# Layer 0 of a hybrid diffusion backbone: modulation dots at other places, convolution tiles in another order, and one scan group in another bank

## The reference, cut to what matters

```
sh1, sc1, g1, sh2, sc2, g2 = split(silu(c) @ ada_w[i] + ada_b[i], 6)
x = layer_norm(ALPHA * x + g1 * mixer(x * (1 + sc1) + sh1))
x = layer_norm(ALPHA * x + g2 * peer_ffn(x * (1 + sc2) + sh2))
```

## Time and profile before

| | |
|---|---|
| Median of three runs | 2045.37 us (2044.3 to 2049.02) |
| Profiled execution | 2046.35 us |
| its span | 2044.5 us |
| mean granted TensorE clock | 0.959 |
| PE busy | 1725.1 us (84%) |
| DVE busy | 1505.0 us (74%) |
| ACT busy | 603.1 us (29%) |
| DMA | 326 GB/s over the span |

### The profile page before, as it was taken

How to read it: one execution, slowest core, us unless ns; L and a number is a source line. 1 busy time by engine, 2 the same in 40 slices (tenths; PEclk the granted TensorE clock), 3 DMA queues, 4 the chain that set the end, 5 groups by cost and what they waited for, 6 DMA issues and landing times.

```text
span 2044.5 us, 18024 instructions
## 1 busy us (share of the span) xinstructions
PE 1725.1 (84%) x5374; PEld 970.2 (47%) x5374; DVE 1505.0 (74%) x3522; ACT 603.1 (29%) x1424; POOL 486.7 (24%) x516
## 2 busy tenths in 40 slices
PE   5998988988789976898899899969788877777776
PEld 5777467765445432343343578645344433332232
DVE  7899995767577767898886576666677777877755
ACT  2654661422222222333232121012222222232221
POOL 0000000003233333343333000013233333333331
PEclk9999998989999999999999899989999999999999
DMA  8244216738999999999999674549999999999996
GB/s 328 85 152 157 83 46 227 270 138 351 420 420 420 418 410 419 363 395 411 408 420 418 264 297 167 201 181 379 419 419 420 414 418 405 395 420 420 419 415 262
DMA packets 94473, 668.13 MB, mean 327 GB/s; under 512 B 11271, under 2 KB 11560, under 8 KB 14504
## 3 DMA queue, kind: packets, MB, share of 16 engines
q0 software_dynamic: 73728, 536.90, 64.2%
q1 hardware_dynamic: 20648, 130.08, 16.8%
HBM read 665.82 MB, written 1.11 MB: 326 GB/s over the span
## 4 chain that ended last, share of the span: by engine, by line
PE 35%; DMA 31%; DVE 15%; issue 2%; ACT 2%; PEldq 0%; POOL 0%; PEld 0%; DVEq 0%; SPq 0%; POOLq 0%; ACTq 0%
DMA expert_rows<-in_p_uv,chosen_experts 30%; PE bank L924 18%; DVE dot_products L1927 5%; PE bank L998 4%; PE bank L892 4%; PE bank L835 2%; PE bank L814 2%; PE bank L1074 1%; ACT weight_diagonal L1325 1%; PE bank L1038 1%; PE bank L1027 1%; DVE modulation_products L1457 1%; DVE scores L1885 1%; PE bank L953 1%; DMA weight_block<-in_m_in_blocks 0%
## 5 line engine op out<-in xcount | busy, mean ns | idle before, releaser
L924 PE MATMUL bank<-expert_rows,weight_diagonal 128*128 128x512 f32 x2048 | 972.6, 619 | 206.7 <-ACT weight_diagonal L1325 205.8
L1927 DVE SCALAR_TENSOR_TENSOR dot_products<-expert_rows,bank 128x1024 f32<-128x1024 f32 x512 | 625.1, 1221 | 314.1 <-DMA expert_rows<-in_p_uv,chosen_experts 304.9
L1103 POOL DMA_INDIRECT expert_rows<-in_p_uv,chosen_experts x512 | 486.5, 950 | 1529.4 <-PE bank L924 819.9
L924 PEld LDWEIGHTS bank<-expert_rows,weight_diagonal 128*128 128x128 f32 x2048 | 384.9, 196 | 733.4 <-issue 391.0
L1316 ACT ACTIVATE expert_gelu<-expert_dots 128x2 f32<-128x2 f32 x256 | 51.9, 203 | 681.6 <-DVE dot_products L1927 681.3
L1325 ACT ACTIVATE weight_diagonal<-constants,expert_weights 128x128 f32<-128x128 f32 x512 | 177.6, 394 | 243.2 <-DVE expert_weights L1859 242.6
L892 PE MATMUL bank<-t_T,weight_block 128*128 128x256 f32 x448 | 108.4, 388 | 10.3 <-DVE t_T L1482 10.3
L892 PEld LDWEIGHTS bank<-t_T,weight_block 128*128 128x128 f32 x448 | 87.4, 196 | 43.7 <-issue 33.8
L730 PE MATMUL bank<-mixer_input_T_hi,weights_hi 128*128 128x512 f32 (+1 forms) x192 | 76.3, 397 | 25.1 <-DVE mixer_input_T_lo L1533 14.8
L998 PE MATMUL bank<-hyena_input_T,hyena_weight_block 128*128 128x256 f32 x384 | 87.3, 389 | 1.8 <-DMA hyena_weight_block<-in_h_in_blocks 1.1
L1625 DVE SCALAR_TENSOR_TENSOR conv_work_or_state<-conv_work_or_state,channel_vectors 128x252 f32<-128x252 f32 (+1 forms) x192 | 82.6, 431 | 4.4
(11 more groups left out here) (260 smaller groups left out, 1901.8 us busy)
## 6 DMA issues: line engine op xcount, KB each, us to landing
weight_block<-in_ada_rows SPq DMA_DIRECT2D x24, 1024.0 KB, 4.8
weight_block<-in_m_in_blocks SPq DMA_DIRECT2D x20, 1024.0 KB, 4.9
weight_block<-in_wq_blocks SPq DMA_DIRECT2D x16, 1024.0 KB, 9.5
hyena_weight_block<-in_ada_rows SPq DMA_DIRECT2D x16, 1024.0 KB, 6.8
hyena_weight_block<-in_h_in_blocks SPq DMA_DIRECT2D x12, 1024.0 KB, 7.2
weight_block<-in_m_out_blocks SPq DMA_DIRECT2D x8, 1024.0 KB, 6.2
expert_rows<-in_p_uv,chosen_experts POOLq DMA_INDIRECT x512, 12.3
hyena_weight_block<-in_h_out_blocks SPq DMA_DIRECT2D x4, 1024.0 KB, 6.3
```

Of the source, the lines that this page charges most:

```text
L924: last = mm(ps[b][:, :], dg[n % DIAG][:, :], uv[slot][:, D + h * 512:D + (h + 1) * 512], start=(r == 0 and k == 0), stop=end)
L1103: pool.indirect_dma_start(uv[slot][:, :], None, A[f"p_uv{l}"], bass.IndirectOffsetOnAxis(ap=chosen[:, s_, k:k + 1], axis=0)).then_inc(uv_l ...
L1927: stt(prod[:, :], uv[slot][:, 0:D], 1.0, rows_t, ALU.mult, ALU.mult, accum_out=dots[:, s_, k + j:k + j + 1]).then_inc(sem("dots_done"), 1)
```

## The change

Two lists and a new order of the tiles replace the fixed formula. C tiles 20 and 21 now stand at q = 12 and 13, tiles 22 and 23 at the end. The ten dots of the convolution stage stand behind tiles 1 to 7, 10, 15 and 17; the two among the weighings are gone. After z block 0 follow four dots, after blocks 1 to 6 two each. Fourteen dots stand in the output projection, one behind each of groups 4 to 15 and two at the end: eight of layer 0 (its last part, with its bias and gate diagonal at group 12) and six of layer 1. The row blocks move in the ring with them. The first weighing is split in four groups, before tiles 16, 18, 20 and 23; the second stands before tile 23. The last `ydiag` uses bank 2. Four groups of output weights are split in the z stage instead of two, the last transposes come before the gate product, which goes to group 14, and SP issues two output blocks ahead of the wait for the filter network's last sine.

```diff
-Z_DOTS = (4, 4, 4, 4, 4, 2, 2, 0)
+Z_DOTS = (4, 2, 2, 2, 2, 2, 2, 0)
+CONV_TILES = (16, 17, 18, 19, 0, 1, 2, 3, 4, 5, 6, 7, 20, 21, 8, 9, 10, 11, 12, 13, 14, 15, 22, 23)
+CONV_WITH_CTX = tuple(q for q, ct in enumerate(CONV_TILES) if ct < CTX_CT)
+CONV_DOTS = (1, 2, 3, 4, 5, 6, 7, 10, 15, 17)
+WEIGH_FIRST = (16, 18, 20, 23)
...
-            plan.use(("ydiag", c, g), 3)
+            plan.use(("ydiag", c, g), 2 if (c, g) == (1, GROUPS - 1) else 3)
...
-    for n, b in enumerate((8, 9, *range(8), 10, 11)):
-        stage("xbc", n, [columns("m_in_blocks", INNER // BLK + b)], lambda n: split_done("xbc", n))
-        if 3 <= n < 11:
-            stage_ada(1, n - 3, n - 2)
+    for n in range(XBC_CT // 2):
+        stage("xbc", n, [columns("m_in_blocks", INNER // BLK + CONV_TILES[2 * n] // 2)], lambda n: split_done("xbc", n))
+        if n in (1, 2, 3, 4, 8):
+            b = (1, 2, 3, 4, 8).index(n)
+            stage_ada(1, b, b + 1)
...
-    stage("mout", 0, [rows("m_out_blocks", b) for b in range(8)], lambda n: split_done("mout", n))
+    for b in range(8):
+        stage("mout", b, [rows("m_out_blocks", b)], lambda n: split_done("mout", n))
+        if 1 <= b < 5:
+            stage_ada(0, 16 + b, 17 + b)
+        elif b >= 5:
+            stage_ada(1, b, b + 1)
...
-        weights(at("z", 0), at("mout", 0))
+        weights(at("z", 0), at("mout", 1) + 1)
...
         for d in range(2):
...
-                pe.wait_ge(sem("x_weighted"), j + 1)
+                if j:
+                    pe.wait_ge(sem("x_weighted"), GROUPS + j)
                 for g in range(GROUPS):
+                    if j == 0:
+                        pe.wait_ge(sem("x_weighted"), g + 1)
...
             if k == 6:
+                normed_transposes(3)
+            elif k == 14:
                 gate_rows(0, 1)
-                normed_transposes(3)
...
-                for q in range(2):
+                for q in range(4):
                     weights_hi("mout", omhi, q, out_used)
...
+        def weigh_first(g):
+
+            for n in (GROUPS + 4 * g + 2, GROUPS + 4 * g + 3):
+                wait_read(dve, ("xT", n))
+            x = slice(g * GW, (g + 1) * GW)
+            tt(weighed[0][:, x].rearrange("p (h d) -> p h d", h=HPG), xtok[:, cols[0][1], x].rearrange("p (h d) -> p h d", h=HPG),
+               bc(wst[:, 0, g * HPG:(g + 1) * HPG], HPG, HD), ALU.mult).then_inc(sem("x_weighted"), 1)
...
-            elif q == CTX_CT + 2:
+            elif q == 14:
                 state_weights()
-                weigh(0)
-            elif q == CTX_CT + 3:
+            if q in WEIGH_FIRST:
+                weigh_first(WEIGH_FIRST.index(q))
+            if q == XBC_CT - 1:
                 weigh(1)
...
-            if 5 <= q < 19:
-                modulation_dot(1, q - 5)
+            if q in CONV_DOTS:
+                modulation_dot(1, CONV_DOTS.index(q))
...
         weigh(2)
-        modulation_dot(1, 14)
         weigh(3)
         weigh(4)
-        modulation_dot(1, 15)
...
-        for k in range(2, INNER // P):
+        for k in range(4, INNER // P):
             if k == 8:
                 normed_lo(3)
             weights_lo(dve, tt, "mout", omhi, omlo, k)
+            if k < 12:
+                modulation_dot(0, 5 * KD + k - 4)
+            else:
+                if k == 12:
+                    modulation_bias(0, 5)
+                    gate_diagonal(0, 1)
+                modulation_dot(1, k - 2)
+        for m in (14, 15):
+            modulation_dot(1, m)
```

More of the change, by code:

```diff
@@ L352, in build_in @@
         plan.use(("xbc", ct), ct % 4)
-        if ct < CTX_CT:
-            plan.use(("xT", ct), 6 + ct % 2)
+    for n in range(CTX_CT):
+        plan.use(("xT", n), 6 + n % 2)
     plan.use("decay", 4)
@@ L377, in build_in @@
         plan.use(("uT", j), 4 + j % 4)
+    for j in (6, 7):
+        plan.use(("uT", j), 4 + j % 4)
     for h in range(2):
         plan.use(("gate", 0, 1, h), 6 + h)
-    for j in (6, 7):
-        plan.use(("uT", j), 4 + j % 4)
     for j in range(4):
@@ L529, in conv_tile @@
     def conv_tile(q):
-        return 16 + q if q < 4 else q - 4 if q < CTX_CT else q
+        return CONV_TILES[q]
     def conv_tap(q, i, j):
@@ L597, in _ @@
         ln_rows(0, 0)
-        weights(at("z", 0), at("mout", 0))
+        weights(at("z", 0), at("mout", 1) + 1)
         sp.wait_ge(sem("sine"), 3)
         sp.dma_start(hdram, hid[:, 0, :]).then_inc(sem("hidden_stored"), 16)
-        weights(at("mout", 0), at(("wq", 0), 4))
+        weights(at("mout", 1) + 1, at(("wq", 0), 4))
         def peer(l):
@@ L724, in _ @@
             b = begin(("xbc", q))
-            c0 = 0 if q < CTX_CT else T
+            c0 = 0 if q in CONV_WITH_CTX else T
             for k in range(KD):
@@ L738, in _ @@
             r = q - 2
-            if 0 <= r < CTX_CT:
+            if r in CONV_WITH_CTX:
+                n = CONV_WITH_CTX.index(r)
                 pe.wait_ge(sem("conv_silu"), r + 1)
-                b = begin(("xT", r))
+                b = begin(("xT", n))
                 for t in range(4):
-                    last = nc.tensor.transpose(ps[b][:, t * P:(t + 1) * P], xc[r % 2][:, t * P:(t + 1) * P], ident)
+                    last = nc.tensor.transpose(ps[b][:, t * P:(t + 1) * P], xc[n % 2][:, t * P:(t + 1) * P], ident)
                 last.then_inc(full[b], 1)
@@ L1192, in _ @@
                 act.wait_ge(sem("conv_done"), r + 1)
[L1193 to L1199, removed]
-                    f(bcT[:, r - CTX_CT + 4, :], cacc[r % 2][:, T:2 * T], ACT.Silu).then_inc(sem("conv_silu"), 1)
+                ct = conv_tile(r)
+                if ct >= INNER // P:
+                    last = f(bcT[:, ct - INNER // P, :], cacc[r % 2][:, T:2 * T], ACT.Silu)
+                if r in CONV_WITH_CTX:
+                    n = CONV_WITH_CTX.index(r)
+                    if n >= 2:
+                        wait_full(act, ("xT", n - 2))
+                    last = f(xc[n % 2], cacc[r % 2], ACT.Silu)
+                last.then_inc(sem("conv_silu"), 1)
             r = q - 2
-            if 0 <= r < 4:
-                copy_out(("xT", r), btok[:, :, r * P:(r + 1) * P], lambda b: b[:, :].rearrange("p (t c) -> p t c", t=4))
-            elif 4 <= r < CTX_CT:
-                copy_out(("xT", r), xtok[:, :, (r - 4) * P:(r - 3) * P], lambda b: b[:, :].rearrange("p (t c) -> p t c", t=4))
+            if r in CONV_WITH_CTX:
+                n, ct = CONV_WITH_CTX.index(r), conv_tile(r)
+                dst = btok[:, :, (ct - INNER // P) * P:(ct - INNER // P + 1) * P] if ct >= INNER // P else xtok[:, :, ct * P:(ct + 1) * P]
+                copy_out(("xT", n), dst, lambda b: b[:, :].rearrange("p (t c) -> p t c", t=4))
         def mask_a(i, d):
@@ L1273, in _ @@
         rms_root(3)
-        for q in range(2, 8):
+        for q in range(4, 8):
             weights_hi("mout", omhi, q, out_used)
-        gate_copy(0, 1)
         normed_hi(3)
@@ L1279, in _ @@
             weights_hi("mout", omhi, q, out_used)
+        gate_copy(0, 1)
         def ln_root(l, j, t):
@@ L1608, in _ @@
             nl = nx = 0
-            ctx_taps = [(1, 0), (1, 2)] if q < CTX_CT else []
+            ctx_taps = [(1, 0), (1, 2)] if q in CONV_WITH_CTX else []
             for i, j in [(1, 0), (1, 2), (0, 1), (2, 1), (0, 0), (0, 2), (2, 0), (2, 2)]:
@@ L1746, in _ @@
             if j == 6:
-                for k in range(2):
+                for k in range(4):
                     weights_lo(dve, tt, "mout", omhi, omlo, k)
@@ L1751, in _ @@
         normalize(3)
-        gate_diagonal(0, 1)
         def ln_stats(l, j, t, keys):
```

2 lines of the change are left out of this document (removed).

## The result

The changed kernel took 2027.81 us (median), the one before 2047.10 in the same series: ratio 0.9907, 95% interval 0.9886 to 0.9928. A second series gave 0.9898 (0.9883 to 0.9914). It is faster by 19.3 us, where 26.9 were forecast; 2027.81 lies 9.3 above the predicted 2018.5 and 0.8 above the upper end of the range. The medians of the second series are 2025.89 and 2047.31, so the same code gained 21.4 us there: whole times tell the gain to about 2 us only.

What follows compares the result with a forecast made beforehand. No engine is full; DVE holds convolution and states and mostly paces the scan, PE waits on z loads and bounds the projection. 4.8 + 9.2 + 8.8 + 4.1 = 26.9 us off gives a median of 2018.5; 8 in 10: 2012.5 to 2027.

Steps and rivals of the forecast that it cites:

- Convolution and states, 4.8: Convolution and context states: fewer dots on DVE, less a late start and new waits, save 4.8 us (bounds 0 and 7 before the states' part).
- The late start at tile 8: Convolution: extra early dots make DVE about 2.5 us later at tile 8, PE's tiles 10 and 11 2.3 to 2.5 later.
- The wait for the transposed copy: Convolution: new wait before tile 23, as the last weighing group needs tile 21's transposed copy from ACT; 1.2 us.
- Rival D: Convolution: short PE waits drop the clock to 1.2 GHz, making the kernel slower than before, 2057 at eight tiles; chance 0.03.
- Last scan group, 9.2: End of scan: bank 2 lets the last products start at 301.5 and run at full pace, first z block too; 9.2 us saved.
- with an idle of 1 us I take 3.68: Last scan group: after only 1 us of idle PE, the last products take 3.68 us instead of 7.06.
- rival B: End of scan: the bank edit doesn't free it; 4.4 us instead of 9.2, 2023.3 in all; chance 0.08.
- z blocks, 8.8: z stage: earlier load issues cut waits from 6.8 to 1.3 us and end slow-clock blocks (3.3); 8.8 us saved.
- Output projection, 4.1: Output projection: 4.4 us wait and 1.7 of slow clock go, 2.1 of new waits come; 4.1 us saved.
- two back to back I take at 7: Output projection: two block loads issued back to back land after 7 us, giving 0.2 + 1.0 us of waits.
- By the pace of PE the seventh block (groups 12, 13) may take 6.2 us to land: Output projection: the seventh projection block's landing may take 6.2 us, the fifth's 6.8, by PE's pace.
- A: Output projection becomes load-bound: at the term's bound of -5 the sum is 17.8 us, 2027.6 in all; chance 0.10.

Runs made afterwards that it cites:

- e6: Changed kernel with the convolution's first seven dots behind tiles 5 to 11 instead of 1 to 7, their loads two pairs later; ratio 0.9892 to the kernel before.
- e1: Changed kernel with the bank edit undone, the last scan group's last diagonal product back in bank 3; ratio 0.9926 to the kernel before.
- e2: Changed kernel with one unneeded 512-column float32 product ahead of the last mixing products' waits; ratio 0.9865 to the kernel before.
- e7: Kernel before with the bank edit alone, the last scan group's last diagonal product in bank 2; ratio 0.9977 to the kernel before.
- e11: Changed kernel with eight unneeded 64-column float32 products ahead of the last mixing products' waits; ratio 0.9893 to the kernel before.
- e4: Changed kernel with the seven row blocks loaded in the output projection cut to a sixteenth of their bytes, same order; ratio 0.9876 to the kernel before.
- e3: Changed kernel with each output block loaded ahead of the row block in the projection, row blocks one step later; ratio 0.9877 to the kernel before.
- e12: Kernel of e9 with each z block loaded ahead of the row blocks of the step before; ratio 0.9884 to the kernel before.
- e9: Changed kernel with e2's product, e3's order, and layer 0's last bias and gate diagonal at group 13 instead of 12; 2016.63 us, ratio 0.9845 to the kernel before.

## Why the prediction was partly wrong

By its own terms, measured up to the end of the projection: 4.9 + 4.4 + 8.9 + 1.3 = 19.5 us, where 4.8 + 9.2 + 8.8 + 4.1 = 26.9 were forecast.

**Convolution and states, 4.8: right.** The first product of the first scan step behind the decay sums starts at 230.82 us, before at 235.73. The third weighing's products come 2.6 us earlier (212.12, 214.72 before) for the 2.5. The late start at tile 8 was passed on: tile 10's products start at 117.81 and 117.53 in the two profiles, before at 114.80, so 2.7 to 3.0 us later where 2.3 to 2.5 were forecast, and e6 shows that 2.1 of it are the early dots'. The wait for the transposed copy was 1.0 us for 1.2. Rival D did not occur; the clock of the stage is 0.98.

**Last scan group, 9.2: wrong, and this is the larger miss.** The step that failed is the sentence "with an idle of 1 us I take 3.68". The start came at the forecast distance, but the products took 6.64 and the first z block 9.1 us instead of 7.1. What remained is the term's own lower bound, 4.4, and the price given to rival B. The reasoning took the slow clock for a consequence of the long wait, so that a short one would be free of it; e1, e2, e7 and e11 show that here 1 us of gap does nearly as much as 5.4, and that the clock stays where the gap is filled. The earlier trace rows had both the 5.39 us and the slow products, and no row with a short gap ahead of them: the value between was chosen where only the two ends were known. Filling the gap brings 4.6 us, and with them the term that was forecast: from the start of the decay products to the end of the second z block it is 22.3 us in e2 and was 31.5 in the kernel before, 9.1 less.

**z blocks, 8.8: right.** 8.9 us; one wait of 1.4 (1.3 forecast) and 7.07 to 7.17 us for each block behind it.

**Output projection, 4.1: the mechanism right, its size wrong.** The wait of 4.4 us and the slow clock behind it went, but against them stand 4.5 us of waits where 2.1 were put down: 1.87 us for 0.2 at group 8, 2.02 for 1.0 at group 12, 0.65 for 0.9 at group 13. (The 1.0 was itself a slip: 7 less 6.2 is 0.8.) The failed step is "two back to back I take at 7". The fifth block took 8.3 us, with the next pair asked for 4.6 us behind its own. The seventh took 6.7, less than the 7. What failed there is "By the pace of PE the seventh block (groups 12, 13) may take 6.2 us to land": it was issued late, because SP waits for DVE's dots and these stood behind the fifth block, so that by the times above (406.50 for the group's start, 2.02 of wait, 2.46 from landing to use) only about 4.7 us were left. e4 shows that bytes are the cause of both waits: the fifth block lands 3 us sooner and the seventh is issued 2.6 to 2.8 us sooner. e3 shows that a block which goes first has enough lead. Why the fifth and sixth took 8.3 and 8.7 us and the seventh and eighth, two pairs just as close, 6.7 and 7.9 (8.2, 8.6, 7.1 and 7.5 in the second profile) stays open. The remaining 0.3 us (4.4 + 1.7 - 4.5 is 1.6, measured 1.3) is within the reading. The prediction named 8 us as the landing that would show it wrong.
The Trainium skill ("DMA: Bandwidth & Descriptors", section Anatomy of one DMA) gives 2.0 us and bytes over 436 GB/s, fitted on transfers that GpSimd issues; these are SyncE's. If the four blocks are taken as one queue from 382.19 on, an estimate by it has the second in place at 389.0 and the fourth at 393.8, 6.4 and 6.7 us behind their issues; the trace has 390.86 and 395.83. So the rule, asked about all four blocks, would still have come out below 7 us and doesn't give the miss.

**Whole time.** The expert stages pass the gain on, as assumed: 19.5 us at the projection's end, 19.3 in the medians. That the two agree so well is partly luck, since the second series gave 21.4. 2045.37, the median that the forecast started from, less 19.5 is 2025.9; the kernel before was itself 1.7 us slower in the series that timed both, and that makes 2027.6. The range was missed by 0.8 us, less than the 1.9 between the medians of the two series; the two misses of 4.8 and 2.8 us behind it are in both profiles. It failed because both lie on one side, and because A and B were given chances as if only one of them could come. B came in full (4.8) and A with 2.8 of its 9.1 us.

## What to carry to other kernels

When a change shortens a wait ahead of short products, ask whether the wait disappears or only shrinks: what remains can cost the clock as the whole did, and one cheap product that nothing needs, put ahead of the wait, shows which it is. One late load can also be paid twice, since what waits for it may hold the issue of the next. When transfers are added to a stage, count the bytes that are in flight when the urgent one is issued, over all its neighbours, and let the urgent one go first; but look at what the deferred one holds up, as in e12.

## What the runs showed of the hardware that was not expected

The granted clock went from 2.4 to 1.2 GHz at the last scan group after 0.96 to 1.01 us without a product, in six of six profiles. Waits as long or longer elsewhere mostly left it alone. These are the second and third weighing's products of the changed kernel:

```profile
206.30 3.70 PE L772 MATMUL bank<-x_weighted,B_tokens 128*128 128x512 f32 x8 [1.07 <-DVE x_weighted L1611]
212.12 3.70 PE L772 MATMUL bank<-x_weighted,B_tokens 128*128 128x512 f32 x8 [2.12 <-DVE x_weighted L1611]
```

In the twelve profiles of the changed kernel and its variants, the wait of 1.07 or 1.08 us never cost the clock, and that of 2.12 once (e6). The kernel before lost it behind a wait of 2.12 us ahead of its second weighing's products (5.40 us, 0.68 granted), e7 did not (3.70). Waits of 1.17 to 1.44 us for z block 2 cost it in one of ten profiles (e9). In the projection waits of 1.7 to 2.5 us left it in both profiles of the changed kernel, and waits of 2.08 and 2.06 us cost it in e6 and e2. So the length of a gap alone doesn't tell whether the clock falls. What else decides was not settled: that the products ahead of the gap in the scan are narrow would fit, but no run changed them, and the narrow filling products kept the clock as well as the wide one.

In e6 a loss of 1.7 us early in the scan came with a gain of 4.1 to 4.3 us at its end, because PE, 1.3 to 1.5 us late there, no longer had a gap to wait in.
